# Compression's inner layer: block rows as the stationary operand, keys and values on two column halves of TensorE, then turned; six bias rows issued from ScalarE's queue

## Chip, cores and metric

One core of a Trainium2 chip runs the whole program in one launch. The metric is device time in microseconds; lower is better. All data is float32; the large products are made in a reduced-precision form of it (fp32r) with high and low parts.

## What is computed

The reference runs two transformer blocks on 256 tokens of width 1024. The change lies in the first layer's attention, in the part that compresses keys and values. A token's keys (and values) have 4 groups of 64. Blocks of 32 tokens, one every 16 tokens, make 15 blocks; each block of a group is a row of 2048 numbers that goes through a two-layer network:

```python
def compress(t, pe, w1, w2):
    blk = t[:, tok_idx] + pe[:, None, :]
    blk = jnp.moveaxis(blk, 3, 2).reshape(B, n_c, N_KV, CMP_BLOCK * HEAD_DIM)
    return jax.nn.gelu(blk @ w1) @ w2

k_cmp = compress(kvh(kc), pe_k, w1_k, w2_k)
v_cmp = compress(kvh(vc), pe_v, w1_v, w2_v)
s = jnp.einsum('bsgrd,bngd->bgrsn', q, k_cmp).astype(jnp.float32) * scale
p, denom, _ = masked_softmax(s + bias_c, dist_c >= 0)
```

So `blk` is 60 rows (4 groups by 15 blocks) of 2048, `w1` is 2048 x 256 and `w2` is 256 x 64, once for keys and once for values. The scores of the compressed keys get a bias by distance, then softmax weights. The same layer has two more attention branches, which use the same bias table, and then its output projection, a feed-forward layer and the rest of the two blocks.

## The kernel before, in words

Every engine has its own instruction stream, written out by hand; semaphores tie them together. The order of the work is the order of the calls in each engine's block. Weights come in units of at most 1 MB. SyncE issues a unit's load (`load_unit`, line 162) into one of three slots, once the unit three before it has been split. ScalarE makes the high part (`split_hi`, L172) when the unit has landed and TensorE has used up the slot's former unit, VectorE the low part (`split_lo`, L180), and TensorE multiplies with three products for each one (`mm3`, L197 to L199). Plain float32 products go through `mm` (L203); the profile shows two loads and two matmuls for each such call. The units of the first projection are called a_in 0 to 10 here: 0 to 5 are the queries, 6 and 7 the keys and values that are compressed and those of the second branch, 8 the gate (192 KB), 9 and 10 the last keys and values. a_out 0 to 3 are the output projection's.

TensorE's stream in `project_a_tensor`: the queries; the products of a_in 6 and 7 (`project_keys_a_tensor`); the compression's inner layer (`compress_hidden_tensor`); the gate; the compressed keys (`compress_keys_tensor`); scores of the first pair of heads (`score_pair_a_tensor`); then a_in 9 in four parts (`project_keys_a_part`) with the compressed scores, the turned gate and the compressed values between them; a_in 10 with a second score pair; the turned compression weights (L1102); and then `attend_a_tensor`, in which the pairs of heads go round between TensorE, VectorE and ScalarE.

The inner layer before: its stationary operand is a 128x128 tile of `w1`, its moving operand the 60 block rows. For keys and then for values there are 16 slices of 128 inputs by 2 halves of the hidden width, 64 calls of `mm` in all. The hidden layer so comes out with the hidden unit on the partitions, as 128 x 120 for the keys in bank 4 and for the values in bank 5. VectorE and ScalarE then make the gelu of each (`gelu_vector`, L1111 to L1121; tanh in `gelu_scalar`, L1126), 120 columns at a time, that of the keys while TensorE is at the values. Ahead of it GpSimd makes the block rows by adding the position terms (L1042, 8 additions), when ScalarE has copied the compressed keys (L990) and VectorE the compressed values (L992) out of PSUM.

VectorE's stream around it: split of a_in 7, the copy L992, split of a_in 8 and 9, the copy L1019, split of a_in 10, the two gelus, the values' hidden layer spread over the heads (L1174), split of a_out 0, the gate (L1024), the compressed scores' bias and softmax (L1185 to L1212) with two pairs of heads between. ScalarE's: the copy of the last queries (L957), split of a_in 7, the copy L990, splits of a_in 8 and 9, the copy L964, split of a_in 10, tanh for the keys, tanh of the gate (L969), the copy of the compressed keys (L1135), tanh for the values, split of a_out 0.

The bias table has 16 rows of heads, each 128 x 256, read by a sliding window from a table in HBM. GpSimd's queue issues 10 of these transfers (L789, 128 KB each) before it makes the block rows and 6 after them; only then it clears the buffers `HID` and `PC` (L1049, L1050), after both halves of the inner layer are made (`a_products_made` 2). `compress_weights_vector` waits for all 16 rows.

Of the kernel before, what the change touches and what calls it, by code (L numbers as in the profile page):

```python
# [17 lines left out]
P = 128  # L18
# [886 lines left out]
def project_a_tensor(pe, m):  # L905

    n = first_unit("a_in")
    src = (m.HTH, m.HTL)
    heads = [head_pair(r) for r in range(4)]
    project_turned_part(pe, m, n, 0, heads, src, 0, 0)  # L910
    tables_tensor(pe, m, (2, 3))
    project_turned_part(pe, m, n, 0, heads, src, 0, 1)
    project_turned(pe, m, n + 2, 2, heads, src)
    pe.wait_ge(m.s("a_left_out"), 1)
    pe.wait_ge(m.s("a_right_out"), 1)
    project_turned(pe, m, n + 4, 0, [cols(j * P) for j in range(4)], src)
    pe.wait_ge(m.s("a_left_out"), 2)
    pe.wait_ge(m.s("a_right_out"), 2)
    project_keys_a_tensor(pe, m, n + 6, 2)
    pe.wait_ge(m.s("tables_copied"), 4)  # L920
    compress_hidden_tensor(pe, m)
    project_gate_a_tensor(pe, m, n + 8)
    compress_keys_tensor(pe, m)
    pe.wait_ge(m.s("a_left_out"), 4)
    pe.wait_ge(m.s("a_right_out"), 4)
    score_pair_a_tensor(pe, m, 0)

    pe.wait_ge(m.s("gelu1_steps"), 1)
# [12 lines left out]

def project_a_scalar(act, m):
# [13 lines left out]
    act.activation(m.A.QT[:, 1, 0:2, :], left(2), ACT.Copy, scale=0.125).then_inc(evac, 1)  # L957
    split_hi(act, m, n + 7)
# [37 lines left out]
def project_a_vector(dve, m):  # L996
# [24 lines left out]
    compress_hidden_vector(dve, m)  # L1021
    split_lo(dve, m, first_unit("a_out"))
# [11 lines left out]
def compress_gpsimd(pool, m):  # L1034
# [4 lines left out]
    for n, (dst, src) in enumerate(((m.A.RK, m.A.KC2), (m.A.RV, m.A.VC2))):  # L1039
        for g in range(KV):  # L1040
            blocks = bass.AP(src.tensor, src.offset + g * S, [list(src.ap[0]), [2, 16], [16, NCMP]])
            ins = pool.tensor_tensor(dst[:, :, g, :], blocks,  # L1042
                                     m.PE[:, n, :].unsqueeze(2).to_broadcast([P, 16, NCMP]), ALU.add)
        ins.then_inc(m.s("blocks_ready"), 1)
    pool.memset(m.A.KCB, 0.0).then_inc(m.s("padding_zero"), 1)
    pool.memset(m.A.SC[:, 0, :, m.ncmp[0]:16], NEG).then_inc(m.s("padding_zero"), 1)
    bias_a_gpsimd(pool, m, range(10, HEADS))
    pool.wait_ge(m.s("a_products_made"), 2)
# [4 lines left out]
def compress_hidden_tensor(pe, m):  # L1053

    pe.wait_ge(m.s("w1_in"), 32)
    for n, (w1, r) in enumerate(((m.A.W1K, m.A.RK), (m.A.W1V, m.A.RV))):
        pe.wait_ge(m.s("blocks_ready"), n + 1)
        for u in range(16):
            for k in range(2):
                ins = mm(pe, m.pb[4 + n][:, k * 64:k * 64 + KV * NCMP], w1[:, u, k * P:(k + 1) * P],  # L1060
                         r[:, u, :, :].rearrange("p g n -> p (g n)"), u == 0 and k == 0, u == 15)
        ins.then_inc(m.s("a_products_made"), 1)

def compress_keys_tensor(pe, m):

    pe.wait_ge(m.s("gelu0_steps"), 6)
    pe.wait_ge(m.consts_in, 16 * m.n_consts)
    for k in range(2):
        ins = mm(pe, m.pb[6][:, 0:60], m.W2[:, 0, k, :], m.A.GH[:, k, 0:60], k == 0, k == 1)  # L1070
    ins.then_inc(m.s("k_cmp_made"), 1)
# [88 lines left out]
def compress_hidden_vector(dve, m):  # L1160

    def hidden(n):
        return m.pb[4 + n][:, 0:P].rearrange("p (k c) -> p k c", k=2)[:, :, 0:60]

    dve.wait_ge(m.s("a_products_made"), 1)
    gelu_vector(dve, m, "gelu0", m.A.GX, m.A.GY, hidden(0), m.A.GH[:, :, 0:60])
    dve.wait_ge(m.s("gelu0_steps"), 6)
    dve.wait_ge(m.s("a_products_made"), 2)
    gelu_vector(dve, m, "gelu1", m.A.GX, m.A.GY, hidden(1), m.A.GX)
    dve.wait_ge(m.s("gelu1_steps"), 6)  # L1170
    dve.wait_ge(m.s("padding_zero"), 3)
    for k in range(2):
        src = m.A.GX[:, k, :].rearrange("p (g n) -> p g n", g=KV)
# [1844 lines left out]
def views(ctx, nc, m):  # L3018
# [76 lines left out]
    A.RK = cut.take(16, KV, NCMP)  # L3095
    A.RV = cut.take(16, KV, NCMP)
# [107 lines left out]
def hybrid_transformer_kernel(nc, i, out):  # L3204
    with ExitStack() as ctx:
# [50 lines left out]
        def _(pool):  # L3256
# [5 lines left out]
            bias_a_gpsimd(pool, m, range(0, 10))  # L3262
# [175 lines left out]
```

## Time and profile before

| | |
|---|---|
| time, median of 3 runs | 1349.34 us (1348.51 to 1350.95) |
| the profiled execution's own time | 1350.74 us |
| its span in the profile | 1348.9 us |
| TensorE matmul busy | 1310.4 us, 97% |
| VectorE, ScalarE, GpSimd busy | 60%, 48%, 19% |
| mean granted clock of TensorE | 0.994 of full speed |
| HBM | 167 GB/s over the span |

The profile follows one execution; times are in us from the start of its span. PE is TensorE's matmuls and PEld its weight loads, DVE VectorE, ACT ScalarE, POOL GpSimd, SP SyncE; a q behind the name is the engine's queue of transfer issues. A busy PE need not be PE at its peak, since matmuls are pipelined. The idle time in brackets is the engine's own, just ahead of the instruction, with what ended it.

### The profile page before, as it was taken

What the parts mean: (1) busy time and instruction counts of PE and PEld (TensorE: products, weight loads), DVE (VectorE), ACT (ScalarE), POOL (GpSimd) and SP (SyncE); (2) the same over time, 40 slices, a digit from 0 to 9 for tenths busy, and PEclk for the clock granted to TensorE, in tenths of its full rate; (3) what the DMA queues carried; (4) which work ended last, traced back from release to release, by engine and by line L of the source; (5) the groups of instructions that cost most, each with busy time, mean ns of one, the idle gap of its engine ahead of it and who ended that gap; (6) DMA issues with size and microseconds to landing.
All of it is one profiled execution on the core that took longest, in us unless ns stands there. A gap on an engine that the chain in (4) does not pass through costs nothing. (4 is left out here: it accounts for less than half of the span.)

```text
span 1348.9 us, 19325 instructions
## 1 busy us (share of the span) xinstructions
PE 1310.4 (97%) x7309; PEld 1092.0 (81%) x7309; DVE 812.8 (60%) x1207; ACT 652.3 (48%) x944; POOL 252.8 (19%) x338
## 2 busy tenths in 40 slices
PE   7999999999899999999999999999999999999997
PEld 5996778888799988788887788888877767788886
DVE  3448665555554486654555755557888766655554
ACT  4328654444443377543444644445443664544442
POOL 5410110000000021102000489502375110100000
PEclk9999999999899999999999999999999999999999
DMA  9980556555355553467654555654535334665550
GB/s 292 255 143 2 155 178 194 187 187 187 125 188 188 157 129 96 164 210 170 230 187 156 173 187 188 219 193 130 188 126 156 105 114 138 199 196 186 190 191 36
DMA packets 155371, 225.82 MB, mean 167 GB/s; under 512 B 12995, under 2 KB 107435, under 8 KB 155308
## 3 DMA queue, kind: packets, MB, share of 16 engines
q1 hardware_dynamic: 141008, 208.88, 49.2%
q0 software_dynamic: 9840, 11.60, 4.3%
q10 hardware_dynamic: 4460, 4.48, 1.0%
q8 instruction: 41, 0.67, 0.2%
q14 instruction: 22, 0.18, 0.0%
HBM read 223.59 MB, written 1.27 MB: 167 GB/s over the span
## 5 line engine op out<-in xcount | busy, mean ns | idle before, releaser
L197 PE MATMUL bank<-units_hi,turned_hi 128*128 128x512 f32 (+1 forms) x840 | 325.4, 387 | 4.5 <-DVE turned_lo L365 1.8
L199 PE MATMUL bank<-units_hi,turned_lo 128*128 128x512 f32 (+1 forms) x840 | 319.4, 380 | 0.0
L198 PE MATMUL bank<-units_lo,turned_hi 128*128 128x512 f32 (+1 forms) x840 | 319.2, 380 | 0.0
L526 DVE TENSOR_TENSOR units_lo<-raw_units,units_hi 128x2048 fp32r<-128x2048 f32 x96 | 222.1, 2313 | 155.0 <-ACT units_hi L480 155.0
L180 DVE TENSOR_TENSOR units_lo<-raw_units,units_hi 128x2048 fp32r<-128x2048 f32 (+2 forms) x103 | 232.0, 2259 | 122.5 <-ACT units_hi L172 122.4
L172 ACT ACTIVATE units_hi<-raw_units 128x2048 fp32r<-128x2048 f32 (+2 forms) x103 | 193.1, 1884 | 122.8 <-PE bank L199 99.3
L480 ACT ACTIVATE units_hi<-raw_units 128x2048 fp32r<-128x2048 f32 x96 | 183.5, 1912 | 104.2 <-PE bank L199 104.2
L197 PE MATMUL bank<-units_hi,second_hi 128*128 128x512 f32 (+1 forms) x576 | 225.0, 391 | 1.7 <-DVE second_lo L2921 1.0
L199 PE MATMUL bank<-units_hi,second_lo 128*128 128x512 f32 (+1 forms) x576 | 222.8, 387 | 0.0
L198 PE MATMUL bank<-units_lo,second_hi 128*128 128x512 f32 (+1 forms) x576 | 222.5, 386 | 0.0
L197 PEld LDWEIGHTS bank<-units_hi,turned_hi 128*128 128x128 f32 x840 | 158.6, 189 | 38.5 <-issue 4.9
L199 PEld LDWEIGHTS bank<-units_hi,turned_lo 128*128 128x128 f32 x840 | 158.5, 189 | 30.7
L198 PEld LDWEIGHTS bank<-units_lo,turned_hi 128*128 128x128 f32 x840 | 158.8, 189 | 28.0
L197 PEld LDWEIGHTS bank<-units_hi,second_hi 128*128 128x128 f32 x576 | 108.2, 188 | 25.7 <-issue 2.4
L199 PEld LDWEIGHTS bank<-units_hi,second_lo 128*128 128x128 f32 x576 | 108.2, 188 | 22.1
L198 PEld LDWEIGHTS bank<-units_lo,second_hi 128*128 128x128 f32 x576 | 108.3, 188 | 21.1
L203 PE MATMUL bank<-arena 128*64 128x128 f32 (+5 forms) x916 | 90.8, 308 | 0.0
L490 ACT ACTIVATE second_hi<-bank 128x512 fp32r<-128x512 f32 x44 | 26.3, 599 | 128.1 <-PE bank L599 128.1
L203 PEld LDWEIGHTS bank<-arena 128*64 128x64 f32 (+2 forms) x916 | 66.6, 163 | 24.4 <-issue 17.2
L532 DVE SCALAR_TENSOR_TENSOR rows<-rows,bank 128x256 f32<-128x256 f32 x88 | 36.8, 418 | 58.0 <-ACT rows L486 42.2
L540 DVE TENSOR_TENSOR second_lo<-bank,second_hi 128x512 fp32r<-128x512 f32 x44 | 30.4, 690 | 67.6 <-ACT second_hi L490 67.6
L197 PE MATMUL bank<-second_hi,units_hi 128*128 128x256 f32 x240 | 68.3, 285 | 0.0
(328 smaller groups left out, 1668.9 us busy)
## 6 DMA issues: line engine op xcount, KB each, us to landing
raw_units<-in_ffn_w_up SPq DMA_DIRECT2D x88, 512.0 KB, 4.7
raw_units<-in_ffn_w_in SPq DMA_DIRECT2D x88, 512.0 KB, 4.7
raw_units<-in_ffn_w_down SPq DMA_DIRECT2D x22, 1024.0 KB, 4.9
raw_units<-in_ffn_w_out SPq DMA_DIRECT2D x22, 1024.0 KB, 4.9
raw_units<-in_w_in SPq DMA_DIRECT2D x18, 1024.0 KB, 5.1
raw_units<-in_b_w_q SPq DMA_DIRECT2D x12, 1024.0 KB, 5.1
raw_units<-in_a_w_in SPq DMA_DIRECT2D x10, 1024.0 KB, 11.7
raw_units<-in_kv_w SPq DMA_DIRECT2D x6, 1024.0 KB, 5.2
```

Source lines behind the costliest of these rows:

```text
L172: act.activation(hi, raw, ACT.Copy).then_inc(m.hi_done, 1)
L180: dve.tensor_tensor(lo, raw, hi.bitcast(F32), ALU.subtract).then_inc(m.lo_done, 1)
L197: pe.matmul(out, lh, rh, start=start, stop=False, skip_group_check=True)
L198: pe.matmul(out, lh, rl, start=False, stop=False, skip_group_check=True)
L199: return pe.matmul(out, ll, rh, start=False, stop=True, skip_group_check=True)
L203: return pe.matmul(out, lhsT, rhs, start=start, stop=stop, skip_group_check=True)
L480: act.activation(m.WH[:, slot(n0 + j), :], m.RAW[:, slot(n0 + j), :], ACT.Copy).then_inc(m.hi_done, 1)
L490: act.activation(turned(m.OTH, s), m.pb[TR_BANK][:, :], ACT.Copy).then_inc(hi, 1)
L526: dve.tensor_tensor(m.WL[:, slot(n0 + j), :], m.RAW[:, slot(n0 + j), :], m.WH[:, slot(n0 + j), :].bitcast(F32), ALU.subtract).then_inc(m.l ...
L532: dve.scalar_tensor_tensor(out=m.UU[:, t, :], in0=m.TH[:, t, :], scalar=1.0, in1=m.pb[t][:, 0:FSTEP], op0=ALU.add, op1=ALU.mult).then_inc( ...
L540: dve.tensor_tensor(turned(m.OTL, s), m.pb[TR_BANK][:, :], turned(m.OTH, s).bitcast(F32), ALU.subtract)\
```

## The change

The operands of the inner layer are swapped. The 60 block rows, padded with zeros to 64, are stationary (128x64), and `w1` is moving, 256 columns at a time. The keys' result goes to partitions 0 to 63 of bank 4 and the values' to partitions 64 to 127, that is, to the two column halves of the array, in alternation. The result is 128 rows (64 of keys, 64 of values) by 256 hidden units, so one gelu of 128x256 serves for both. Two transposes and one copy then bring it to the form that the next layer takes. GpSimd issues 10 bias rows and ScalarE the other 6, between the copy of the last queries and the split of a_in 7. GpSimd clears `HID` and `PC` after `a_products_made` 1.

```diff
+POOL_ROWS = 10
+def bias_a_gpsimd(pool, m):
     pool.wait_ge(m.s("tables_stored"), 80)
-    for h in heads:
+    for h in range(POOL_ROWS):
+        pool.dma_start(*bias_a_row(m, h)).then_inc(m.s("bias_a_in"), 16)
+
+def bias_a_scalar(act, m):
+    act.wait_ge(m.s("tables_stored"), 80)
+    for h in range(POOL_ROWS, HEADS):
+        act.dma_start(*bias_a_row(m, h)).then_inc(m.s("bias_a_late_in"), 16)
@@ project_a_tensor
     compress_hidden_tensor(pe, m)
     project_gate_a_tensor(pe, m, n + 8)
-    compress_keys_tensor(pe, m)
+    hidden_turn_tensor(pe, m)
     pe.wait_ge(m.s("a_left_out"), 4)
     pe.wait_ge(m.s("a_right_out"), 4)
     score_pair_a_tensor(pe, m, 0)
-
-    pe.wait_ge(m.s("gelu1_steps"), 1)
+    compress_keys_tensor(pe, m)
@@ project_a_scalar
     act.activation(m.A.QT[:, 1, 0:2, :], left(2), ACT.Copy, scale=0.125).then_inc(evac, 1)
+    bias_a_scalar(act, m)
     split_hi(act, m, n + 7)
@@ project_a_vector
     compress_hidden_vector(dve, m)
+    spread_hidden_vector(dve, m)
     split_lo(dve, m, first_unit("a_out"))
@@ compress_gpsimd
     for n, (dst, src) in enumerate(((m.A.RK, m.A.KC2), (m.A.RV, m.A.VC2))):
+        pool.memset(dst[:, :, :, NCMP:16], 0.0)
...
-    bias_a_gpsimd(pool, m, range(10, HEADS))
-    pool.wait_ge(m.s("a_products_made"), 2)
+    pool.wait_ge(m.s("a_products_made"), 1)
     pool.memset(m.A.HID, 0.0).then_inc(m.s("padding_zero"), 1)
@@ compress_hidden_tensor
-    for n, (w1, r) in enumerate(((m.A.W1K, m.A.RK), (m.A.W1V, m.A.RV))):
-        pe.wait_ge(m.s("blocks_ready"), n + 1)
-        for u in range(16):
-            for k in range(2):
-                ins = mm(pe, m.pb[4 + n][:, k * 64:k * 64 + KV * NCMP], w1[:, u, k * P:(k + 1) * P],
-                         r[:, u, :, :].rearrange("p g n -> p (g n)"), u == 0 and k == 0, u == 15)
-        ins.then_inc(m.s("a_products_made"), 1)
+    pe.wait_ge(m.s("blocks_ready"), 2)
+    for u in range(16):
+        for n, (w1, r) in enumerate(((m.A.W1K, m.A.RK), (m.A.W1V, m.A.RV))):
+            ins = mm(pe, m.pb[4][n * DH:(n + 1) * DH, 0:S], r[:, u, :, :].rearrange("p g n -> p (g n)"), w1[:, u, :],
+                     u == 0, u == 15)
+    ins.then_inc(m.s("a_products_made"), 1)
+
+def hidden_turn_tensor(pe, m):
+    pe.wait_ge(m.s("gelu0_steps"), 6)
+    for k in range(2):
+        ins = pe.transpose(m.pb[5][:, k * P:(k + 1) * P], m.A.GX[:, k * P:(k + 1) * P], m.IDENT[:, :])
+    ins.then_inc(m.s("a_products_made"), 1)
@@ compress_keys_tensor
-    pe.wait_ge(m.s("gelu0_steps"), 6)
+    pe.wait_ge(m.s("hidden_copied"), 1)
     pe.wait_ge(m.consts_in, 16 * m.n_consts)
     for k in range(2):
-        ins = mm(pe, m.pb[6][:, 0:60], m.W2[:, 0, k, :], m.A.GH[:, k, 0:60], k == 0, k == 1)
+        ins = mm(pe, m.pb[6][:, 0:DH], m.W2[:, 0, k, :], m.A.GH[:, k, 0, :], k == 0, k == 1)
@@ compress_keys_scalar
     ins.then_inc(m.s("k_cmp_ready"), 1)
-    gelu_scalar(act, m, "gelu1", m.A.GY)
@@ compress_hidden_vector
     dve.wait_ge(m.s("a_products_made"), 1)
-    gelu_vector(dve, m, "gelu0", m.A.GX, m.A.GY, hidden(0), m.A.GH[:, :, 0:60])
-    dve.wait_ge(m.s("gelu0_steps"), 6)
+    gelu_vector(dve, m, "gelu0", m.A.GX, m.A.GY, m.pb[4][:, 0:S], m.A.GX)
     dve.wait_ge(m.s("a_products_made"), 2)
-    gelu_vector(dve, m, "gelu1", m.A.GX, m.A.GY, hidden(1), m.A.GX)
-    dve.wait_ge(m.s("gelu1_steps"), 6)
+    dve.tensor_copy(m.A.GH, m.pb[5][:, 0:S].rearrange("p (k n c) -> p k n c", k=2, n=2))\
+        .then_inc(m.s("hidden_copied"), 1)
+
+def spread_hidden_vector(dve, m):
+    dve.wait_ge(m.s("hidden_copied"), 1)
     dve.wait_ge(m.s("padding_zero"), 3)
@@ compress_weights_vector
-    dve.wait_ge(m.s("bias_a_in"), 16 * HEADS)
+    dve.wait_ge(m.s("bias_a_in"), 16 * POOL_ROWS)
+    dve.wait_ge(m.s("bias_a_late_in"), 16 * (HEADS - POOL_ROWS))
```

## Rows read from the trace of the kernel before

**Rows 1.** The page: its span, and TensorE's busy time

```profile
span 1348.9 us, 19325 instructions
PE 1310.4 (97%) x7309; PEld 1092.0 (81%) x7309; DVE 812.8 (60%) x1207; ACT 652.3 (48%) x944; POOL 252.8 (19%) x338
```

**Rows 2.** Timeline of TensorE: start, us, what, count, idle ahead of it

```profile
66.82 14.39 PE L203 MATMUL bank<-rows,arena 128*128 128x60 f32 x128
...
83.81 1.41 PE L203 MATMUL bank<-arena 128*128 128x60 f32 x12
85.15 0.39 PE L197 MATMUL bank<-turned_hi,units_hi 128*128 128x256 f32 x1
```

**Rows 3.** Groups of weight loads, 66.8 to 82: busy us, mean ns, idle before

```profile
L203 PEld LDWEIGHTS bank<-rows,arena 128*128 128x128 f32 x128 | 14.4, 191 | 0.0
```

**Rows 4.** Timeline of the weight loads of one attention step, on two column halves

```profile
109.74 0.20 PEld L203 LDWEIGHTS bank<-arena 128*64 128x64 f32 x4 [0.39 <-issue]
...
110.01 0.14 PEld L203 LDWEIGHTS bank<-arena 128*64 128x64 f32 x2
...
110.23 0.14 PEld L203 LDWEIGHTS bank<-arena 128*64 128x64 f32 x2
```

**Rows 5.** Timeline of GpSimd

```profile
60.79 5.76 POOL L1042 TENSOR_TENSOR rows<-arena 128x240 f32<-128x240 f32 x8 [16.44 <-DVE arena L992]
66.49 0.16 POOL L1045 MEMSET arena<- 128x64 f32 x1
...
89.90 0.79 POOL L789 DMA_DIRECT2D tables<-distance_tables  x1 [19.20 <-issue]
```

**Rows 6.** Timeline of VectorE: a_in 10's split, first gelu's ends, the spread

```profile
72.30 2.29 DVE L180 TENSOR_TENSOR units_lo<-raw_units,units_hi 128x2048 fp32r<-128x2048 f32 x1 [2.87 <-ACT units_hi L172]
74.51 0.28 DVE L1111 COPY arena<-bank 128x120 f32<-128x120 f32 x1
...
76.30 0.28 DVE L1121 TENSOR_TENSOR arena<-arena 128x120 f32<-128x120 f32 x1
...
91.75 1.12 DVE L1174 COPY rows<-arena 128x240 f32<-128x240 f32 x2 [6.06 <-POOL rows L1049]
```

**Rows 7.** Groups of wider instructions, 0 to 125: busy us, mean ns, idle before

```profile
L1199 DVE TENSOR_TENSOR arena<-arena 128x480 f32<-128x480 f32 x1 | 0.7, 658 | 0.0
...
L1323 DVE TENSOR_SCALAR arena<-arena 128x256 f32<-128x256 f32 (+1 forms) x29 | 7.4, 318 | 0.3
...
L1357 ACT ACTIVATE arena<-arena 128x256 f32<-128x256 f32 (+1 forms) x35 | 15.6, 450 | 3.4 <-DVE arena L1305 3.4
```

**Rows 8.** Timeline of ScalarE: the splits of a_in 7 and of a_in 10

```profile
53.61 1.92 ACT L172 ACTIVATE units_hi<-raw_units 128x2048 fp32r<-128x2048 f32 x1 [3.34 <-DMA raw_units<-in_a_w_in]
...
70.35 1.91 ACT L172 ACTIVATE units_hi<-raw_units 128x2048 fp32r<-128x2048 f32 x1 [2.74 <-DMA raw_units<-in_a_w_in]
```

**Rows 9.** Timeline of issues on ScalarE's queue: 128 rows of 512 B; 2 MB

```profile
0.73 0.42 ACTq L700 DMA_DIRECT2D ident<-in_c_ident  x1
...
26.96 3.72 ACTq L725 DMA_DIRECT2D arena<-in_a_w_v  x1
```

**Rows 10.** Transfers, 36 to 62, in 40 slices: GB/s

```profile
GB/s 348 348 347 353 359 362 369 367 321 286 277 286 289 266 253 263 242 231 230 242 221 190 193 223 193 160 129 150 133 146 134 150 197 257 260 234 247 222 251 256
```

**Rows 11.** TensorE later: busy by stretch (PE first); timeline: compressed values, third score pair

```profile
90.00:100.00 10.00, 10.00 (x85) 9.68 (x85) 8.01 (x21) 2.28 (x9) 2.54 (x3) 1.00 0.36 95
...
95.00 1.90 PE L203 MATMUL bank<-arena,rows 128*128 128x64 f32 x16
...
104.54 0.92 PE L203 MATMUL bank<-arena 64*128 64x256 f32 x8
```

**Rows 12.** Stretch 363.3 to 373.5 (PEclk third from last); TensorE after two waits

```profile
363.30:373.50 10.20, 8.31 (x36) 7.51 (x37) 7.04 (x12) 7.68 (x18) 0.78 (x2) 0.50 0.00 0
...
363.56 0.48 PE L284 MATMUL bank<-ident,rows 128*128 128x128 f32 x1 [2.23 <-DVE rows L260]
...
755.93 0.47 PE L197 MATMUL bank<-units_hi,turned_hi 128*128 128x512 f32 x1 [1.50 <-DVE rows L535]
```

More of the change, by code:

```diff
@@ L783, in tables_gpsimd, with bias_a_row @@
     pool.dma_start(m.TD[0, :, W_ALL:W_ROW], m.TAB16[:, O_ODD:O_ODD + W_STEP]).then_inc(m.s("tables_stored"), 16)
-def bias_a_gpsimd(pool, m, heads):
+POOL_ROWS = 10
+def bias_a_row(m, h):
+    return m.BIAS[:, h, :], sliding(m.TD, h * W_ROW + O_NAT + 127, 1, [[1, S]])
+def bias_a_gpsimd(pool, m):
     pool.wait_ge(m.s("tables_stored"), 80)
-    for h in heads:
-        pool.dma_start(m.BIAS[:, h, :], sliding(m.TD, h * W_ROW + O_NAT + 127, 1, [[1, S]]))\
-            .then_inc(m.s("bias_a_in"), 16)
+    for h in range(POOL_ROWS):
[4 more added lines that the diff above has]
+        act.dma_start(*bias_a_row(m, h)).then_inc(m.s("bias_a_late_in"), 16)
 def project_turned(pe, m, n, bank, tiles, src, norm=None, between=None):
@@ L1039, in compress_gpsimd @@
     for n, (dst, src) in enumerate(((m.A.RK, m.A.KC2), (m.A.RV, m.A.VC2))):
+        pool.memset(dst[:, :, :, NCMP:16], 0.0)
         for g in range(KV):
             blocks = bass.AP(src.tensor, src.offset + g * S, [list(src.ap[0]), [2, 16], [16, NCMP]])
-            ins = pool.tensor_tensor(dst[:, :, g, :], blocks,
+            ins = pool.tensor_tensor(dst[:, :, g, 0:NCMP], blocks,
                                      m.PE[:, n, :].unsqueeze(2).to_broadcast([P, 16, NCMP]), ALU.add)
@@ L1131, in compress_keys_scalar @@
     act.wait_ge(m.s("padding_zero"), 1)
-    src = m.pb[6][:, 0:60].rearrange("p (g n) -> p g n", g=KV)
+    src = m.pb[6][:, 0:DH].rearrange("p (g n) -> p g n", g=KV)
     for par in range(2):
         rows = slice(par * DH, (par + 1) * DH)
-        ins = act.activation(m.A.KCB[rows, :, par, 0:NCMP], src[rows, par::2, :], ACT.Copy)
+        ins = act.activation(m.A.KCB[rows, :, par, 0:NCMP], src[rows, par::2, 0:NCMP], ACT.Copy)
     ins.then_inc(m.s("k_cmp_ready"), 1)
-    gelu_scalar(act, m, "gelu1", m.A.GY)
 def compress_weights_scalar(act, m):
@@ L1160, in compress_hidden_vector @@
 def compress_hidden_vector(dve, m):
-    def hidden(n):
-        return m.pb[4 + n][:, 0:P].rearrange("p (k c) -> p k c", k=2)[:, :, 0:60]
     dve.wait_ge(m.s("a_products_made"), 1)
-    gelu_vector(dve, m, "gelu0", m.A.GX, m.A.GY, hidden(0), m.A.GH[:, :, 0:60])
-    dve.wait_ge(m.s("gelu0_steps"), 6)
+    gelu_vector(dve, m, "gelu0", m.A.GX, m.A.GY, m.pb[4][:, 0:S], m.A.GX)
     dve.wait_ge(m.s("a_products_made"), 2)
-    gelu_vector(dve, m, "gelu1", m.A.GX, m.A.GY, hidden(1), m.A.GX)
-    dve.wait_ge(m.s("gelu1_steps"), 6)
+    dve.tensor_copy(m.A.GH, m.pb[5][:, 0:S].rearrange("p (k n c) -> p k n c", k=2, n=2))\
+        .then_inc(m.s("hidden_copied"), 1)
+def spread_hidden_vector(dve, m):
+    dve.wait_ge(m.s("hidden_copied"), 1)
     dve.wait_ge(m.s("padding_zero"), 3)
     for k in range(2):
-        src = m.A.GX[:, k, :].rearrange("p (g n) -> p g n", g=KV)
+        src = m.A.GH[:, k, 1, :].rearrange("p (g n) -> p g n", g=KV)[:, :, 0:NCMP]
         ins = dve.tensor_copy(m.A.HID[:, k, :, :, 0:NCMP], src.unsqueeze(2).to_broadcast([P, KV, 4, NCMP]))
@@ L3074, in views @@
     A.CD = cut.take(TT, HEADS)
-    A.GX = cut.take(2, 60)
-    A.GY = cut.take(2, 60)
-    A.GH = cut.take(2, 60)
+    A.GX = A.VCR.rearrange("p g d -> p (g d)")
+    A.GY = cut.take(S)
+    A.GH = cut.take(2, 2, DH)
     A.NM = cut.take(NPA, 2, 2)
@@ L3094, in views @@
     cut = Cutter(rows, 0)
-    A.RK = cut.take(16, KV, NCMP)
-    A.RV = cut.take(16, KV, NCMP)
+    A.RK = cut.take(16, KV, 16)
+    A.RV = cut.take(16, KV, 16)
     cut = Cutter(rows, 0)
@@ L3261, in _ @@
             tables_gpsimd(pool, m)
-            bias_a_gpsimd(pool, m, range(0, 10))
+            bias_a_gpsimd(pool, m)
             compress_gpsimd(pool, m)
```

## The prediction, written before the changed kernel was timed

> **What bounds the kernel now.** I read the page first. TensorE is busy 97% of the span [rows 1], so a shorter stage on it shortens the whole, as long as TensorE does not wait for the difference elsewhere. Then TensorE's timeline from 50 to 110, to find the stage. The 64 calls of the inner layer are 128 passes in 14.39 us, 0.112 us each [rows 2]. The groups of weight loads show why a pass of only 60 columns costs that: each has its own 128-column load, and loads fill the 14.4 us with no idle time [rows 3]. The stage is bound by loads. Last the neighbours: who releases TensorE at 66.8, what VectorE does at 74.5 (the gelu), and what follows to 105.
>
> **The inner layer.** The swap leaves 32 calls, 64 passes of 256 columns. The attention step shows the same form, 128x64 stationary and 256 columns moving, in alternation on two column halves. There the loads come two at a time, at 110.01 and again at 110.23 [rows 4]: a pair of passes costs 0.22 us, where the ramp at the start took 0.27 (109.74 to 110.01). 32 pairs by 0.217 is 6.95 us. Two changes of array shape add about 0.1 us each (estimate: from 0.39 us of issue idle ahead of the first load in [rows 4], of which most is the work before). The stage falls from 14.4 to about 7.15 us. Bounds: 32 by 0.27 is 8.6 us; if the load of a pair (0.14 us in [rows 4]) came on top of its passes, 32 by 0.357 is 11.4 us; with no overlap of the halves at all, 64 by 0.217 is 13.9 us. I take 0.217, since it is the steady step of the same form.
>
> The Trainium skill has a rule against this, on the page "TensorE: Matmul & The Clock Gate", section "Part 3: Packing small matmuls — row/col tiling": a weight load overlaps a running matmul only if the two use different row groups, and the two column halves here share all rows. By that rule it would be the case of 11.4 us; the trace disagrees, with pairs 0.22 us apart although each load takes 0.14.
>
> **Start of the stage.** TensorE now waits for the values' block rows too. GpSimd finishes the 8 additions at 66.55 [rows 5], and two clears of 64 columns (0.16 us for that size [rows 5], two of them, partly pipelined) are put before them. Start: 0.2 us later (bounds 0.1 and 0.4). The stage then ends at 66.82 + 0.2 + 7.1 = 74.1. The gate follows, 2.75 us (from about 81.05, the end of the 128 passes less the last one's tail, to 83.81 [rows 2]), and ends at 76.9.
>
> **The gelu.** Before, the keys' gelu lay under the values' products. Now one gelu comes after everything, and the gate's 2.75 us are its only cover. The old chain of 120 columns ran from 74.51 to 76.58, 2.07 us [rows 6]. At 256 columns: the copy out of PSUM and three multiplications at 0.42 each (between 0.28 for 120 columns [rows 6] and 0.66 for 480 [rows 7]), two scalings at 0.32, tanh at 0.45 [rows 7], and about 0.3 of hand-overs: 3.1 us (bounds 2.9 and 3.4). Its start is the later of 74.1 and VectorE's split of a_in 10, which ends at 74.51 [rows 6].
>
> **The turn.** It waits for the gelu, and behind that wait stands all of TensorE's stream, first the score pair, which needs nothing from it. Two passes (0.25 us), the copy of 0.42 us that lies beside the first score pair's 0.9, then the keys' 4 passes: 14 passes for 12, and two more changes of shape. Before, 83.81 to 85.15, 1.35 us [rows 2]; now 1.65.
>
> **Six bias rows on ScalarE.** Issue: 0.42 us for 128 pieces, the nearest row, or 3.72 us, the farthest, which came behind 2 MB on the same queue [rows 9]; six make 2.5 or 22 us. I take 2.5 to 3, since by then the queue has had 20 us to empty. ScalarE is idle for 3.34 us there, until a_in 7 lands at 53.61 [rows 8], which covers 0.55 us each; at 3.72 the stage would start 19 us late, which is left to the tail.
>
> The transfers are another matter. Their 768 KB used to go after 66.7; now they are in the way from about 52, beside a_in 7 to 9 and the ten rows on GpSimd's queue, while the transfer engines run at 130 to 260 GB/s [rows 10]. a_in 7 is nearly in by then (0 to 0.5 us later). a_in 9 and 10 queue behind: 768 KB at 348 GB/s, the rate of the first slices, is 2.2 us; at 190 it is 4.0 [rows 10]. ScalarE waited for a_in 10 until 70.35 [rows 8] and VectorE's split hangs on it, so nothing covers this. I take 2.2 us, because in the fast slices ScalarE's queue was moving `w1`, in the same pieces of 1 KB. The split of a_in 10 then ends at 76.7, the gelu at 79.8, and TensorE waits 2.9 us from 76.9. If nothing is late: gelu from 74.55 to 77.65, a wait of 0.75 us.
>
> **What comes after.** The first part of a_in 9 started at 85.15 [rows 2]. Now: 79.8 + 1.65 = 81.45, a gain of 3.7 us. From there to 104.5 TensorE is full [rows 11]. The spread (L1174) must be ready for the compressed values, which came at 95.00 [rows 11]. It was held by GpSimd's sixteenth issue: 19.2 us of waiting until 89.90 [rows 5], VectorE idle 6.06 us until 91.75 [rows 6]. It had 2 us of room, less than the gain; with the rows moved the spread is done at about 82, for a use at 91.3. The compressed softmax starts once TensorE has turned the gate, so it moves along with TensorE and, with VectorE no longer held, by more: covered. GpSimd's clears (2 us from 74.1) lie under the gelu. So the whole 3.7 us reach the third score pair [rows 11], and the attention loop, bound by VectorE and ScalarE, starts that much earlier. Nothing later is tied to a fixed time.
>
> **The sum** against the profiled execution (1350.74 us; the span 1348.9 and 1.8 around it): +0.2 start, -7.25 stage, +2.9 wait, +0.3 turn, about -3.8, by the timeline -3.7: 1347.0. The median of the runs is 1.4 below that execution, so 1345.6 for the median.
>
> **Rivals.** (R1) The transfers are not late, because the engines take the 1 KB pieces into gaps. The wait is 0.75 us, the gain 5.85, the time 1343.5. For it: 348 GB/s were possible shortly before. Against: the engines were busy throughout.
>
> (R2) Slower: the clock. TensorE's wait of 2.23 us at 363.56 stands in a stretch that ran at 0.50, 1.2 GHz, for 10.2 us from 363.3; the waits of 1.50 us and less left it at 2.4 GHz [rows 12]. A new wait of 2.9 us is longer. If the clock falls there for as long, up to 5.1 us are lost to passes at half rate: -3.7 + 5.1 = +1.4, 1350.8. It decides once the new wait is as long as that of 2.23 us, 0.7 less than I expect; if the clock is low for a third of that time, the result is 1348.7. With a_in 10 four us late it would be 1352.6. The same page of the Trainium skill, section "Part 1: The HAM clock gate", says that low activity puts the clock back to half; by that the trace agrees.
>
> (R3) The change does not do what it says, the halves do not run side by side over a long stretch. At 13.9 us the stage ends at 81.1, the gelu at 84.2, and 1.65 us on it is 85.85: 0.7 slower, 1350.0. Against it are [rows 4], though they show only two such pairs in a row.
>
> (R3b) Load and passes of a pair add up, 11.4 us: the stage ends at 78.6, the gelu at 81.7, 1.8 us faster, 1347.5. Against it is the same step of 0.22 us. This is what the rule of "TensorE: Matmul & The Clock Gate" quoted above would make of it.
>
> (R4) a_in 7 is held up. Behind it hang its low part, the copy L992 and GpSimd's additions, which had 0.3 us of room before TensorE's start. Late by 4 us it gives 1347.3; by 2 us nothing, since a_in 10 is later.
>
> **Chances.** Forecast 0.38; R1 0.25; R2 0.22; R3 0.03; R3b 0.03; R4 0.07; anything else 0.02. A measurement of this kernel can tell about 0.2%, 2.7 us, from no change. Faster: the forecast and R1, less the part of the forecast at 3 to 4 us late: 0.62. Slower: R2 at its worst with a longer wait, and part of the rest: 0.07. Same: 0.31. The range reaches from R1 with 0.9 us on top (no late start, a shorter gelu, 1342.6) to most of R2 and R3 (1349.9); outside are the clock's full price and the tail of the issues.
>
> **What would show it.** TensorE: 64 passes of 128x256 in 7 us from 67.0 (R3: 11 to 14), and a wait ahead of the two transposes of 2.9 us, put down to VectorE's L1121 (R1: under 1 us). ScalarE: its wait for a_in 10 ends at 72.5, not 70.35; six issues of 0.4 to 0.5 us end before 53.6. GpSimd: no 19 us wait, VectorE's idle time before the spread gone. Granted clock 1.00 up to 100 (R2: 0.5 in a stretch from about 79). The third score pair at 100.8. I am wrong if that pair starts earlier and the end does not follow, or if the stage itself takes over 9 us.

## The result, and the profile after

The changed kernel takes 1368.12 us (median of 4 runs, 1366.25 to 1368.21) against 1349.21 for the kernel before (4 runs, 1348.51 to 1350.95): 1.0130 times as long, 95% interval 1.0118 to 1.0142, or 19 us slower. The forecast was 1345.6 with a range to 1349.9. The profiled execution took 1368.19, its span is 1366.4 us, 17.5 more than before.

ScalarE's timeline, the issues on its queue with it, shows where it begins (start, us; in brackets the idle time ahead and what ended it):

```profile
48.76 8.52 ACTq L803 DMA_DIRECT2D tables<-distance_tables  x3
...
57.31 14.90 ACTq L803 DMA_DIRECT2D tables<-distance_tables  x3
72.31 1.91 ACT L172 ACTIVATE units_hi<-raw_units 128x2048 fp32r<-128x2048 f32 x1 [21.16 <-issue]
```

The first line is three of the six issues, the second the other three. One by one they last 0.61, 0.60, 7.25, 6.17, 6.05 and 2.63 us: 23.3 us together, against the 2.5 to 3 of the forecast. The split of a_in 7 stands behind them on the same engine. It started at 53.61 before [rows 8]; now it starts at 72.31, and the releaser is "issue", not the transfer: the unit, issued at 38.26, had landed 16.1 us later, at 54.3.

The waits from 40 to 125 (in total, times, longest) show who stood behind that split:

```profile
POOL rows L1055 <- DVE arena L1006: 35.0, 1, 35.0
DVE units_lo L180 <- ACT units_hi L172: 34.8, 5, 20.7
...
PE bank L197 <- DVE units_lo L180: 15.0, 1, 15.0
...
PE bank L203 <- POOL rows L1058: 3.1, 1, 3.1
```

TensorE stands for 15.0 us ahead of a_in 7's products, then 3.1 us until GpSimd has made the block rows that come out of them. About 2.0 of the 3.1 are one addition, at 80.45, that ran beside VectorE's split of a unit and took 2.77 us; the others take 0.7. The stretches (length, busy time of PE, PEld, DVE, ACT, POOL with counts, granted clock, DMA share, GB/s) add the second cost:

```profile
61.60:76.60 15.00, 0.00 (x1) 0.00 (x0) 2.34 (x3) 4.23 (x6) 0.00 (x0) 0.56 0.18 60
76.60:84.40 7.80, 7.76 (x48) 7.56 (x48) 5.96 (x7) 2.26 (x3) 4.94 (x5) 0.74 0.82 230
...
87.50:96.20 8.70, 8.70 (x65) 5.63 (x65) 1.96 (x1) 0.00 (x0) 0.07 (x1) 0.81 0.97 210
...
68.00:76.00 8.00, 0.00 (x0) 0.00 (x0) 1.74 (x1) 3.65 (x5) 0.00 (x0) 0.50 0.14 48
```

In the wait the clock falls to 1.2 GHz, from 63.5 to 80.6, so that a_in 7's products run their first 4.0 us at half rate; it falls again from 87.4 to 90.8. The timeline of TensorE, for [rows 2] and [rows 11]:

```profile
87.45 8.79 PE L203 MATMUL bank<-arena,rows 128*64 128x256 f32 x64 [3.09 <-POOL rows L1058]
100.06 0.44 PE L1083 MATMUL bank<-ident,arena 128*128 128x128 f32 x2 [0.87 <-DVE arena L1143]
...
121.12 0.92 PE L203 MATMUL bank<-arena 64*128 64x256 f32 x8
```

The inner layer starts 20.6 us late (87.45 against 66.82): 15.0 and 3.1 of waiting and 2.0 of half clock make 20.1 of it. It takes 8.79 instead of 14.39 us, with 3.4 us of it at half clock. The third score pair comes 16.6 us late (121.12 against 104.54), and the end 17.5.

### The profile page after: what moved, and what is told of

Same layout as the page of the kernel before. It is cut to its first block and busy times, and to the rows that moved or that the text cites. A ratio compares the mean times of both kernels' runs of the same rounds, so it can differ in the third digit from the quotient of the medians.

```text
span 1366.4 us, 19195 instructions
## 1 busy us (share of the span) xinstructions
PE 1307.0 (96%) x7247; PEld 1086.1 (79%) x7247; DVE 814.5 (60%) x1202; ACT 652.3 (48%) x943; POOL 249.0 (18%) x334
## 3 DMA queue, kind: packets, MB, share of 16 engines
q10 hardware_dynamic: 5240, 5.27, 1.2%
## 5 line engine op out<-in xcount | busy, mean ns | idle before, releaser
L203 PE MATMUL bank<-arena 128*64 128x128 f32 (+4 forms) x916 | 90.9, 308 | 0.0
L197 PE MATMUL bank<-turned_hi,units_hi 128*128 128x256 f32 (+1 forms) x184 | 55.4, 301 | 18.5 <-DVE units_lo L180 15.0
## 6 DMA issues: line engine op xcount, KB each, us to landing
raw_units<-in_a_w_in SPq DMA_DIRECT2D x10, 1024.0 KB, 10.2
```

Of the source, the lines that this page charges most:

```text
L197: pe.matmul(out, lh, rh, start=start, stop=False, skip_group_check=True)
L203: return pe.matmul(out, lhsT, rhs, start=start, stop=stop, skip_group_check=True)
```

## The experiments

The first pair asks which part of the change costs the time.

**The six rows back on GpSimd**, the rest of the change kept:

```diff
@@ project_a_scalar
-    bias_a_scalar(act, m)
@@ compress_gpsimd
+    for h in range(POOL_ROWS, HEADS):
+        pool.dma_start(*bias_a_row(m, h)).then_inc(m.s("bias_a_late_in"), 16)
     pool.wait_ge(m.s("a_products_made"), 1)
```

> The change without its part on ScalarE: GpSimd issues the last six bias rows where it did before. Theory A (the loss of 19 us is ScalarE held up by its six issues of up to 7.2 us; the new inner layer gains): no issue on ScalarE, a_in 7 split at 53.6 again, the 64 passes in about 7.1 us at the full clock, the gelu from 74.5 to 77.6. GpSimd's sixteenth issue then holds the clear of HID and with it the spread to about 92, so TensorE waits ahead of the compressed values: about 2 us gained on before, 1347.3 (1346 to 1348.5). Theory B (the new inner layer itself costs, by a low clock or by passes that do not run side by side): above 1352, and the 64 passes take 9 us or more.

Measured: 1349.49 us (11 runs, 1345.50 to 1351.16), before 1350.14 (23 runs), ratio 0.9990, interval 0.9981 to 0.9999; the profiled execution 1346.94. All 19 us are gone. TensorE's timeline:

```profile
67.19 7.15 PE L203 MATMUL bank<-arena,rows 128*64 128x256 f32 x64 [1.42 <-POOL rows L1057]
...
99.93 0.92 PE L203 MATMUL bank<-arena 64*128 64x256 f32 x8 [0.65 <-ACT arena L991]
```

The stage is the forecast's, 7.15 us, and in this execution the third pair is 4.6 us earlier. The long wait at GpSimd's sixteenth issue, which I expected again, did not come (six issues in 4.8 us from 67.22 on). The median keeps only 0.6 us; the runs scatter over 5.7 us, and what takes the gain back in most of them was not found. One lead: already in this fast execution VectorE waits for the last bias rows, which are issued late.

```profile
91.53 0.83 DVE L1209 TENSOR_TENSOR arena<-bank,tables 128x112 f32<-128x112 f32 x2 [3.03 <-DMA tables<-distance_tables]
```

The kernels below that gain have no such wait. Whether it grows in the slower executions is not shown, since none of them was traced.

**The kernel before with only the six rows on ScalarE's queue**:

```diff
@@ project_a_scalar
     act.activation(m.A.QT[:, 1, 0:2, :], left(2), ACT.Copy, scale=0.125).then_inc(evac, 1)
+    bias_a_scalar(act, m)
     split_hi(act, m, n + 7)
@@ compress_gpsimd
-    bias_a_gpsimd(pool, m, range(10, HEADS))
```

(Left out here: the function itself and the matching waits of `compress_weights_vector`.)

> The kernel before with only the six rows moved to ScalarE's queue, in the place that the change gives them (counted on a semaphore that is otherwise used up by then). Theory A: the same 20 us hold before a_in 7's split, TensorE waits 15 us in the products of a_in 7, and the time is 1366 to 1372, as the old inner layer's 7 us are kept. Theory B: within 3 us of before.

Measured: 1368.10 us (4 runs), ratio 1.0137, interval 1.0123 to 1.0152. The waits:

```profile
ACT units_hi L172 <- issue: 21.1, 1, 21.1
...
PE bank L197 <- DVE units_lo L180: 14.7, 1, 14.7
```

The same two waits as after the change, without the new inner layer. The six issues (0.61, 0.61, 7.13, 5.25, 7.03, 2.61 us) alone cost 18 us here (1368.10 against 1350.14), as expected.

**Why an issue is held.** Next to be asked was what an issue waits for. A row reads its source in the form 2 x 64 x 256. The third row was the first to be held. In the stretch from 68 to 76 after the change (the last row of the stretches above) nothing moves but these rows. The share of 16 transfer engines is 0.14, that is 2.2 engines, at 48 GB/s, while ScalarE's issues are held until 72.2. At that rate a row of 128 KB takes 2.7 us, and the sixth issue took 2.63. The issues of 6 to 7 us lie earlier, where other transfers run beside the rows: from 52 to 66 ScalarE's queue moved only 0.16 MB, 11 GB/s. Three kernels change the form. They read the late rows from 16, 4 or 8 copies of their tables, stored by one more transfer, so that the outermost step of a row has so many entries; bytes, pieces (1 KB) and place are those of the change:

```diff
@@ tables_gpsimd
+    pool.dma_start(m.TL.rearrange("c h w -> h c w"),
+                   m.TAB16[POOL_ROWS:HEADS, 0:W_NAT].unsqueeze(1).to_broadcast([HEADS - POOL_ROWS, 16, W_NAT]))\
+        .then_inc(m.s("tables_stored"), 16)
...
+def bias_a_row_spread(m, h):
+    i = h - POOL_ROWS
+    return m.BIAS[:, h, :], bass.AP(m.TL.tensor, i * W_NAT + 127, [[6 * W_NAT - 8, 16], [-1, 8], [1, S]])
@@ bias_a_scalar
-        act.dma_start(*bias_a_row(m, h)).then_inc(m.s("bias_a_late_in"), 16)
+        act.dma_start(*bias_a_row_spread(m, h)).then_inc(m.s("bias_a_late_in"), 16)
```

**16 entries:**

> The change, but ScalarE's six rows read a table of 16 copies (one more small transfer stores it), so that the outermost step of each source has 16 entries where it had 2. Theory A1 (a transfer whose outermost step has two entries runs on two of the transfer engines, 64 pieces on each, and the third such issue finds their queues full): each issue takes 0.6 us, the rows land within some 5 us, none of it holds ScalarE, and the time is 1344 to 1347. Theory A2 (ScalarE's queue stalls because of the other traffic at 50 to 70 us, whatever the pattern): issues of 3 us and more stay, 1360 and above.

Measured: 1348.04 us (12 runs, 1345.85 to 1357.10), ratio 0.9997, interval 0.9983 to 1.0011; 1344 to 1347 had been expected. No issue over 0.81 us:

```profile
47.65 1.94 ACTq L811 DMA_DIRECT2D tables<-late_tables  x3
...
49.62 2.18 ACTq L811 DMA_DIRECT2D tables<-late_tables  x3
53.12 1.92 ACT L172 ACTIVATE units_hi<-raw_units 128x2048 fp32r<-128x2048 f32 x1 [3.08 <-DMA raw_units<-in_a_w_in]
...
72.54 1.91 ACT L172 ACTIVATE units_hi<-raw_units 128x2048 fp32r<-128x2048 f32 x1 [4.56 <-DMA raw_units<-in_a_w_in]
```

```profile
66.40 7.15 PE L203 MATMUL bank<-arena,rows 128*64 128x256 f32 x64 [0.57 <-POOL rows L1066]
...
79.64 0.44 PE L1091 MATMUL bank<-ident,arena 128*128 128x128 f32 x2 [3.20 <-DVE arena L1151]
```

This is the forecast's own case at last: a_in 10 split at 72.54, a wait of 3.20 us ahead of the turn. The clock then stands at 1.2 GHz from 80.96 to 84.37, and the third pair comes at 102.24. The six issues last 4.0 us together, more than the 3.34 us of idle time that the forecast set against them, and still cost ScalarE nothing: they start at 47.65, beside the split of a_in 6 and the copy behind it.

**4 entries:**

> As the one before, with 4 copies: 4 entries, 32 pieces on each of four engines per transfer, 192 for the six. Theory A1, with room for 128 pieces or a little more on an engine's queue (two of 64 went in at once, the third did not): four issues of 0.6 us, the fifth or sixth held for 1 to 3 us; time 1345 to 1350. If the limit is a number of transfers and not of pieces (two at once): the third issue is held again, 1355 and above.

Measured: 1358.98 us (4 runs), ratio 1.0067, interval 1.0050 to 1.0084. Issues of 0.62, 0.52, 0.53, 0.67, 11.63 and 1.38 us: four pass, the fifth is held, for 11.6 us and not the 1 to 3 expected; so the time misses its 1345 to 1350.

```profile
48.18 2.44 ACTq L811 DMA_DIRECT2D tables<-late_tables  x4
...
50.65 13.03 ACTq L811 DMA_DIRECT2D tables<-late_tables  x2
63.78 1.91 ACT L172 ACTIVATE units_hi<-raw_units 128x2048 fp32r<-128x2048 f32 x1 [13.21 <-issue]
```

```profile
65.00:68.00 3.00, 0.00 (x0) 0.00 (x0) 2.28 (x3) 2.94 (x6) 0.00 (x0) 0.67 0.27 97
```

With nothing else moving the share is 0.27, or 4.3 engines, and 97 GB/s: twice that of two entries.

**8 entries:**

> The change with the six late rows in a form whose outermost step has 8 entries, in the change's own place on ScalarE's queue (a copy of the six tables is read, as in the form with 16). By the theory that a row is dealt to as many transfer engines as its outermost step has entries, and that ScalarE's queue holds about 128 pieces per engine in flight, a row puts 16 pieces on each of 8 engines, six rows 96: under 128, so none of the six issues is held up, each 0.5 to 0.9 us; ScalarE splits a_in 7 at about 53 and the inner layer starts at 66 to 67. Rival 1 (the room is one in bytes or in transfers, and four entries were held at the fifth because four rows were in flight): the fifth issue takes 3 us or more again, and TensorE waits ahead of the inner layer. Rival 2 (any form below 16 entries is slow enough to hold the sixth): one issue of 2 us or more. Time: by the first theory 1346 to 1350, near the form with 16 entries (1348.04) and perhaps 1 us above it, as the rows take longer on half of the engines and a_in 9 and 10 may land later; by rival 1 near the form with 4 (1359).

Measured: 1354.28 us (5 runs), ratio 1.0031, interval 1.0017 to 1.0046. The issues are 0.69, 0.59, 0.58, 0.58, 0.74 and 2.95 us: the sixth is held, which the second rival had and the count of 128 pieces had not. It costs nothing here (a_in 7 split at 53.25). What costs is a_in 10:

```profile
67.91 1.91 ACT L172 ACTIVATE units_hi<-raw_units 128x2048 fp32r<-128x2048 f32 x1 [8.16 <-DMA raw_units<-in_a_w_in]
...
78.45 1.91 ACT L172 ACTIVATE units_hi<-raw_units 128x2048 fp32r<-128x2048 f32 x1 [8.01 <-DMA raw_units<-in_a_w_in]
```

**Fewer rows on ScalarE**, two in the old form, and 14 early ones on GpSimd:

```diff
-POOL_ROWS = 10
+POOL_ROWS = 14
```

> The changed kernel with 14 rows on GpSimd, all ahead of the block rows, and 2 on ScalarE, in the two-entry form. By theory A1 with room for 128 pieces on an engine's queue: 2 issues of 0.6 us each, no stall, a_in 7's split at 53 to 54, time 1345 to 1349. If the stall came from the pattern itself or from the traffic: at least one issue above 2 us and 1355 or more. GpSimd's queue may itself be full at the 14 (its 16th issue waited 19 us before): then GpSimd starts the block rows late and the stage begins after 67.

Measured: 1359.17 us (4 runs), ratio 1.0057, interval 1.0037 to 1.0076. The two issues take 0.61 and 0.59 us, as expected. The time was a miss: ScalarE now waits for the units.

```profile
ACT units_hi L172 <- DMA raw_units<-in_a_w_in: 31.3, 5, 9.9
...
PE bank L1083 <- DVE arena L1143: 10.4, 1, 10.4
```

a_in 10 is split from 80.11 on, the turn waits 10.4 us, and the clock is at half from 81.0 to 104.9. Fourteen of a_in 10's 16 completions are there by 72.9, the last two at 79.0 and 80.1: two engines are late, as many as a row in the old form is on. Which of the rows hold them, GpSimd's four more or ScalarE's two, is not shown.

**The spread rows, later.** To take away the late a_in 10 too, the six issues (16 entries) go behind its split:

```diff
@@ project_a_scalar
-    bias_a_scalar(act, m)
     split_hi(act, m, n + 7)
...
     split_hi(act, m, n + 10)
+    bias_a_scalar(act, m)
     gelu_scalar(act, m, "gelu0", m.A.GY)
```

> As e3 (16 entries), but ScalarE issues the six rows behind the split of a_in 10, not ahead of that of a_in 7. Theory C (in e3 the rows' 768 KB in the way of a_in 8 to 10 made TensorE's wait ahead of the turn 3.20 us, and that wait brought the clock down for 3.4 us): a_in 10 is split from about 70.4 again, the gelu begins at 74.5, the wait ahead of the turn is about 1 us, the granted clock stays at 1.00 from 20 to 350, and the third score pair starts at about 99.4 where e3 had 102.2; median 3 us below e3. Theory D (a_in 10 is late for another reason, such as the extra table): wait of 2.5 us or more, time as e3.

Measured: 1345.99 us (9 runs, 1345.23 to 1349.43), before 1349.85 (27 runs), ratio 0.9975, interval 0.9966 to 0.9985: faster than both kernels, by 3.9 us against the one before.

```profile
68.10 7.15 PE L203 MATMUL bank<-arena,rows 128*64 128x256 f32 x64 [1.11 <-POOL rows L1066]
79.06 0.44 PE L1091 MATMUL bank<-ident,arena 128*128 128x128 f32 x2 [0.93 <-DVE arena L1151]
...
100.11 0.92 PE L203 MATMUL bank<-arena 64*128 64x256 f32 x8
```

The clock stays full from 21.8 to 359.7. The third pair is 4.4 us earlier than before, the span 4.7 shorter: what is gained here reaches the end. The wait of 1.11 us ahead of the inner layer is a new one. a_in 9 comes earlier, VectorE's split of it (64.40 to 66.71) falls beside GpSimd's additions, and one of these takes 2.76 us in place of 0.73.

**The score pair first, the clears later.** In the kernel above one scaling of the gelu takes 1.10 us and its twin 0.29. VectorE, and GpSimd beside it:

```profile
76.21 1.10 DVE L1145 TENSOR_SCALAR arena<-arena 128x256 f32<-128x256 f32 x1
...
78.25 0.29 DVE L1149 TENSOR_SCALAR arena<-arena 128x256 f32<-128x256 f32 x1 [0.48 <-ACT arena L1156]
...
75.31 0.95 POOL L1072 MEMSET rows<- 128x1024 f32 x1 [7.11 <-PE bank L203]
76.21 0.95 POOL L1073 MEMSET arena<- 128x1024 f32 x1
```

The long one runs beside a clear of 1024 columns. So:

```diff
@@ project_a_tensor
-    hidden_turn_tensor(pe, m)
     pe.wait_ge(m.s("a_left_out"), 4)
     pe.wait_ge(m.s("a_right_out"), 4)
     score_pair_a_tensor(pe, m, 0)
+    hidden_turn_tensor(pe, m)
@@ compress_gpsimd
-    pool.wait_ge(m.s("a_products_made"), 1)
+    pool.wait_ge(m.s("gelu0_steps"), 6)
```

> As e5, with the first score pair ahead of the turn, where it needs nothing from the gelu, and GpSimd's two clears held until the gelu is done. Theory E (GpSimd's clears keep VectorE from its shared way to SBUF: one scaling of the gelu took 0.98 us in e1 and 1.10 in the changed kernel, 0.29 where no clear ran): the scaling takes 0.29 us beside it, the gelu 3.1 us from its start, TensorE has no wait over 0.3 us ahead of the turn, and the third score pair starts another 0.9 to 1.5 us earlier than in e5. Against it: the clears now end later and the spread waits for them, which costs nothing as long as they end before the compressed values.

Measured: 1346.12 us (12 runs), ratio 0.9976, interval 0.9963 to 0.9988.

```profile
75.83 0.29 DVE L1145 TENSOR_SCALAR arena<-arena 128x256 f32<-128x256 f32 x1
...
77.88 0.95 POOL L1072 MEMSET rows<- 128x1024 f32 x1 [10.05 <-DVE arena L1151]
```

The scaling is back at 0.29 us, and TensorE waits for nothing ahead of the turn. In the profile the third pair is 0.74 us earlier (99.37). The medians, 0.1 us apart, can't tell the two kernels apart.

**All keys, then all values**, in the kernel with the late spread rows:

```diff
@@ compress_hidden_tensor
-    for u in range(16):
-        for n, (w1, r) in enumerate(((m.A.W1K, m.A.RK), (m.A.W1V, m.A.RV))):
+    for n, (w1, r) in enumerate(((m.A.W1K, m.A.RK), (m.A.W1V, m.A.RV))):
+        for u in range(16):
```

> As e5, but the inner layer makes all 16 slices of the keys and then all 16 of the values, so that neighbours in the stream use the same column half. If the two halves run side by side only because they alternate: 64 passes in 13.7 to 14 us in place of 7.15, and about 6.5 us on e5. If the array is bound by something else (loads, or the moving operand): the same 7.15 us and the time of e5.

Measured: 1350.81 us (10 runs), ratio 1.0008, interval 0.9997 to 1.0019.

```profile
67.80 13.24 PE L203 MATMUL bank<-arena,rows 128*64 128x256 f32 x64 [1.21 <-POOL rows L1066]
```

The same 64 passes take 13.24 us, 0.207 each, where in alternation a pair takes 7.15 / 32 = 0.223. In this form the two column halves do run side by side, but only if neighbours in the stream are on different halves. The third pair moves by 5.8 us (105.92), the median by 4.8.

**All 16 rows over 16 engines.** If rows packed on two engines hold up the units, GpSimd's ten should gain by the new form too. First with ScalarE's six in the change's place, then with them behind a_in 10:

```diff
@@ bias_a_gpsimd
-        pool.dma_start(*bias_a_row(m, h)).then_inc(m.s("bias_a_in"), 16)
+        pool.dma_start(*bias_a_row_spread(m, h)).then_inc(m.s("bias_a_in"), 16)
```

> The change with all 16 bias rows, GpSimd's ten too, read from 16 copies of the tables in the form whose outermost step has 16 entries; places as in the change (six on ScalarE's queue ahead of a_in 7's split). It is the form-of-16 kernel (1348.04, a_in 10 split at 72.5, 3.2 us of waiting ahead of the turn) with GpSimd's ten rows changed as well. Theory: what makes a_in 9 and 10 late is that rows packed on two engines (14 early rows on GpSimd: a_in 10 at 80.1; six rows over 8 engines: 78.5) slow the slowest engine that a 1 MB unit waits for; then with GpSimd's rows also over 16 engines a_in 8 and 9 land 1 to 4 us earlier than 60.7 and 65.4, a_in 10 by 71 or earlier, and the wait ahead of the turn is under 2 us: 1345 to 1347. Rival: GpSimd's queue cuts its rows in another way in any case (its packets are of 4 KB, ScalarE's of 1 KB), the form changes nothing there, or smaller pieces make it slower: a_in 10 at 72.5 or later, 1348 or more. The tables' copies (16 by 16 rows instead of 16 by 6) are stored before the rows start and may move them back by under 2 us, which should cost nothing.

> As the kernel with all 16 rows in the form of 16 entries, but with ScalarE's six after its split of a_in 10 (where the form-of-16 rows for ScalarE alone gave 1345.99, with TensorE waiting 1.1 us ahead of the inner layer and 0.9 ahead of the turn). Theory: as TensorE has no wait on transfers left in that kernel, an earlier a_in 8 to 10 changes nothing: within 1 us of 1345.99; the inner layer 7.15 us again. Rival: the ten rows' form matters before 66 (a_in 6 and 7 land earlier, 52.5 instead of 54, so that the block rows are made earlier and the 1.1 us wait goes): 1344 to 1345.

Measured: 1354.73 us (6 runs), ratio 1.0033, interval 1.0021 to 1.0045; and 1353.50 us (8 runs), ratio 1.0028, interval 1.0017 to 1.0038. Both expectations of the time missed. ScalarE in the first:

```profile
57.42 1.91 ACT L172 ACTIVATE units_hi<-raw_units 128x2048 fp32r<-128x2048 f32 x1 [6.08 <-DMA raw_units<-in_a_w_in]
...
68.26 1.90 ACT L172 ACTIVATE units_hi<-raw_units 128x2048 fp32r<-128x2048 f32 x1
```

a_in 10 does come 4.3 us earlier (68.26 against 72.54), as expected. But a_in 7 comes 4.3 us later (57.42 against 53.12), and behind it stand GpSimd's block rows: TensorE waits 6.84 us ahead of the inner layer (6.43 in the second), and the clock falls to half for 10.2 us (6.8). About 4.1 of the 6.84 come from two additions of the block rows that fall beside VectorE's splits and take 2.75 us each.

The ten rows, 128 KB each, now land 8.1 us after their issue (median), where they took 17.0 with only ScalarE's rows spread:

```profile
tables<-distance_tables POOLq DMA_DIRECT2D x10, 128.0 KB, 17.0
...
tables<-late_tables POOLq DMA_DIRECT2D x10, 128.0 KB, 8.1
```

From 44 to 52 GpSimd's queue moves 1.15 MB in place of 0.44, and the queue of the units 0.81 MB in place of 1.11. So the ten rows go through at the expense of the units; in the old form they are slow, and that leaves room for a_in 7. How much of the delay is due to this alone isn't shown, for two more things differ: the copy of all the tables puts the first row's issue off by 3.4 us (39.98 against 36.55), and GpSimd's queue moves its rows in 224 fewer packets each (8320 and 6080 on the pages).

## Why the prediction was wrong

**The step that failed** is the size of ScalarE's six issues. "Six bias rows on ScalarE" took 0.42 us each from the nearest of two rows far apart, "since by then the queue has had 20 us to empty", and left the case "at 3.72 the stage would start 19 us late" to the tail. Measured were 23.3 us for the six. The reason was wrong too: the queue had not emptied. The second half of `w1`, issued on it 21 us before the rows, was still on its way, and the trace of the kernel before could have told (size, then us from issue to landing; before and after the change):

```profile
arena<-in_a_w_v ACTq DMA_DIRECT2D x1, 2048.0 KB, 25.6
...
arena<-in_a_w_v ACTq DMA_DIRECT2D x1, 2048.0 KB, 26.7
```

It was issued at 27.35 and landed at 54.0; 15 of its 16 completions had come by 49.8, and 22 of its pieces were open when the first row was issued. This remainder is not what held ScalarE, though: the first two issues took 0.6 us, and with 16 entries 75 of its pieces were open and no issue was held. What I missed is that the six fill the queue themselves: each puts its 128 pieces on two transfer engines (share 0.14 of 16; 0.27 with four entries), and other transfers slow them down (11 GB/s beside these, 48 alone). The upper bound was sized right, since six at 3.72 are 22 us, and so was the delay priced from it: 19 against 20.6. Wrong was the chance that I gave it, and with it the upper end of the range.

The Trainium skill has the rule that would have told it, on the page "DMA: Bandwidth & Descriptors", section "Why a DMA increments its semaphore by 16 and not by 1": a transfer is dealt over the largest number of engines up to 16 that divides the slowest dimension of both its patterns, and on ScalarE's queue these are the lowest-numbered ones. For a source of 2 x 64 x 256 that is 2, for all six rows the same two. The trace agrees on the number, with 2.2 engines' worth and the packets counted above; which engines they are it does not show.

**The other steps**, read where the issues don't hide them:
- Inner layer 7.15 us: 7.15 in all kernels that ran it at full clock. The rule on loads, which gave 11.4, does not hold in this form; 13.24 came only without alternation.
- Start of the stage, +0.2 (bounds 0.1 and 0.4): 67.19 with the rows on GpSimd, +0.4; 68.10 in the best kernel, +1.3, where an addition ran beside VectorE's split.
- Gelu 3.1 us (2.9 to 3.4): 2.9 where nothing is beside it. Where the clears run beside it, 3.6 with the rows on GpSimd and 3.7 in the best kernel. "GpSimd's clears lie under the gelu" was wrong: they lengthen it by 0.7 to 0.8 us.
- Transfers late by 2.2 us: with 16 entries a_in 10 was split at 72.54, forecast 72.5, and the wait was 3.20 us, forecast 2.9. In the changed kernel it can't be seen, since a_in 7 is later than all of it. That pieces of 1 KB move as w1's did holds only for this form; over 8 engines a_in 10 came at 78.45.
- Turn 1.65 us: 1.69 both with the rows on GpSimd (78.15 to 79.84) and in the best kernel (79.06 to 80.75).
- R2: a wait of 3.20 us was followed by 3.4 us of half clock and 1348.04. The 1348.7 that R2 gave to a third of the low stretch is a slip: by R2's own sum it is -3.7 + 1.7, or 1347.3 for the median. Measured was 2.1 us below the kernel before (1350.14 in that comparison), but with an interval that includes no change. In the changed kernel the mechanism came with a far longer wait.
- R1, its 0.75 us of waiting: 0.93 in the best kernel, but only because the rows are issued later. R3 is excluded in the changed order. R4, a_in 7 held up, was the mechanism's place; I saw it as a slow transfer, not as an engine that stands still ahead of the split of a unit that has landed.
- "The end follows": a third pair 4.4 us earlier, a span 4.7 shorter in the best kernel.

**What stays open:** why the median with the rows back on GpSimd keeps 0.6 us of a gain of 4; why GpSimd's sixteenth issue, held for 19 us before, was not held there; and in what ScalarE's queue counts its room (below). The six rows in the old form behind a_in 10 were not tried.

## What to carry to other kernels

A transfer issued from an engine that also computes is an instruction in that engine's stream: price it by the one that finds its queue full, and look at who stands behind it, for a short idle gap covers only short issues. Whether the queue is empty by then is read from when its earlier transfers landed, not from when they were issued. Read a transfer's pattern for the number of engines that it goes to; the same bytes over 2, 4, 8 and 16 engines gave 1368, 1359, 1354 and 1348 us here. And when every transfer is made wide, the early ones may crowd out the one that the critical path waits for (1354.73 us, a cause that is in part argued): first decide which transfer may be slow.

## What the runs showed of the hardware

- **Room on ScalarE's queue.** Pieces per transfer engine that had been issued ahead of the first issue held: 128 in the form of two entries (third row, 7.2 us), 128 with four (fifth row, 11.6 us), but 80 with eight (sixth row, 2.95 us); with 16 entries six rows, 48 pieces, passed. The first two fit a room of 128 pieces, the third doesn't, not even with what was left of `w1` then (6 pieces in all): the count is not settled.
- **A unit waits for its slowest engines, and narrow rows make some engines slow.** With equal bytes, six rows over 8 engines or over 16 put a_in 10's split at 78.45 or 72.54. Its completions tell why: with rows over 8, eight of the 16 are late (by 69.5, from 73.1 on); with old rows over 2, two are (by 72.9, then 79.0 and 80.1). That the late ones are the engines of the rows is inferred from these counts; the records name no engine.
- **GpSimd beside VectorE.** A clear of 128x1024 running beside a one-input scaling in float32 stretched it from 0.29 to 1.10 us; its neighbours with two inputs kept 0.42. The Trainium skill, "SBUF — State Buffer", section "SBUF: two separate sides", has the two engines share a pair of ports as an exclusive lock when VectorE is in a two-port mode; the trace agrees in direction, 0.81 us more for a clear of 0.95. Apart from that, an addition of block rows (128x240, 0.72 us on GpSimd) beside VectorE's split of a unit (2.3 us) took 2.75 to 2.77 us: at 80.45 after the change, at 64.52 in the best kernel.
- **The clock.** TensorE's waits of 2.74, 3.09, 3.20, 6.43, 6.84, 6.88, 8.60 and 10.4 us went with 3.4, 3.4, 3.4, 6.8, 10.2, 6.8, 10.2 and 24 us at 1.2 GHz, the 15.0 us with 17; those from 6.43 us on saw the clock fall while they lasted. Waits of 1.42 us and less, in this part of the program, went with none.
